# Section boundaries of a two-network kernel rebuilt: early modulation sums, GpSimd held back, first units fed by parts of h

## The reference

```python
def first_block(x, c, ...):
    cond = jax.nn.silu(c)
    for l in range(2):
        m = (cond @ w_mod[l] + b_mod[l]).reshape(bsz, 3, 3, 1024)   # shift, scale, gate for 3 sublayers
        x = x + 0.5 * m[:, 0, 2] * swiglu(adaln_in(x, norm_g[l, 0], m, 0), w1, w3, w2)   # d_ff 2752
        h = adaln_in(x, norm_g[l, 1], m, 1) @ w_in[l]
        mix = mixer_ab(h, ...) if l % 2 == 0 else mixer_cd(h, ...)
        x = x + m[:, 1, 2] * (mix @ w_out[l])
        x = x + 0.5 * m[:, 2, 2] * swiglu(adaln_in(x, norm_g[l, 2], m, 2), w1, w3, w2)

def second_block(x, c, ...):
    for l in range(2):
        sh_m, sc_m, g_m, sh_f, sc_f, g_f = split(silu(c) @ w_mod[l] + b_mod[l], 6)
        x = x + g_m * mixer(rms_norm(x) * (1 + sc_m) + sh_m, ...)
        x = x + g_f * moe_ffn(rms_norm(x) * (1 + sc_f) + sh_f, ...)   # 64 experts of width 256, top 8, and a shared one
```

## Time and profile before

| | us |
|---|---|
| median of 3 runs | 4393.25 |
| lowest and highest | 4388.53, 4394.18 |
| span of the profiled execution | 4386.6 |
| PE busy in it | 4127.6 (94%) |
| DVE, ACT, POOL busy | 2587.6, 1470.3, 990.2 |

### The profile page before, as it was taken

One profiled execution on the slowest core, in us unless ns is written; L12 is line 12 of the kernel. 1 busy time (PEld: TensorE's weight loads), 2 busy tenths in 40 slices (PEclk: granted clock), 3 DMA queues, 4 the chain that ended last, 5 costly groups with the idle time before them and its releaser, 6 DMA issues.

```text
span 4386.6 us, 74944 instructions
## 1 busy us (share of the span) xinstructions
PE 4127.6 (94%) x29877; PEld 3940.1 (90%) x29877; DVE 2587.6 (59%) x3637; ACT 1470.3 (34%) x2008; POOL 990.2 (23%) x640
## 2 busy tenths in 40 slices
PE   4998998987999888999999999998899999999999
PEld 2996898975998777999999999987789999999999
DVE  6754576655755645855555555547345555555555
ACT  1332333321331132333333333311323333333333
POOL 3827465552737104500000000061000000000000
PEclk9999898998999998999999999999989999999999
DMA  6765575752766324765656556563235565565654
GB/s 239 245 197 177 176 248 187 238 187 76 242 222 211 125 83 138 257 194 185 191 191 188 190 189 190 192 219 115 85 118 182 189 196 184 189 194 185 190 192 140
DMA packets 569485, 804.84 MB, mean 183 GB/s; under 512 B 20973, under 2 KB 487860, under 8 KB 568100
## 3 DMA queue, kind: packets, MB, share of 16 engines
q1 hardware_dynamic: 514364, 665.69, 47.2%
q0 software_dynamic: 31104, 113.26, 7.9%
q10 hardware_dynamic: 23912, 24.44, 1.7%
HBM read 802.13 MB, written 1.20 MB: 183 GB/s over the span
## 4 chain that ended last, share of the span: by engine, by line
PE 87%; DVE 10%; ACT 1%; issue 1%; DMA 1%; SPq 0%; ACTq 0%; DVEq 0%
PE bank L728 23%; PE bank L729 23%; PE bank L730 23%; PE bank L802 9%; DVE work L1785 3%; PE bank L1010 2%; PE bank L722 1%; DVE pb L1696 1%; PE bank L712 1%; DMA ring<-in_w_mod 0%; DVE h L1525 0%; PE bank L996 0%; DVE work L1639 0%; DMA ring<-in_ffn_w 0%; PE bank L824 0%
## 5 line engine op out<-in xcount | busy, mean ns | idle before, releaser
L728 PE MATMUL bank<-hh,hi 128*128 128x256 f32 (+1 forms) x5568 | 1588.5, 285 | 32.2 <-DVE h_lo L1545 30.1
L729 PE MATMUL bank<-h_lo,hi 128*128 128x256 f32 (+1 forms) x5568 | 1585.0, 285 | 0.0
L730 PE MATMUL bank<-hh,ring_lo 128*128 128x256 f32 (+1 forms) x5568 | 1584.7, 285 | 0.0
L728 PEld LDWEIGHTS bank<-hh,hi 128*128 128x128 f32 (+1 forms) x5568 | 1073.3, 193 | 38.6 <-DVE h_lo L1545 24.2
L729 PEld LDWEIGHTS bank<-h_lo,hi 128*128 128x128 f32 (+1 forms) x5568 | 1074.3, 193 | 0.0
L730 PEld LDWEIGHTS bank<-hh,ring_lo 128*128 128x128 f32 (+1 forms) x5568 | 1073.9, 193 | 0.0
L1556 DVE TENSOR_TENSOR ring_lo<-ring,hi 128x1024 fp32r<-128x1024 f32 (+1 forms) x696 | 861.1, 1278 | 76.8 <-ACT hi L1141 76.7
L728 PE MATMUL bank<-hid,hi 128*128 128x256 f32 (+1 forms) x2784 | 789.0, 283 | 3.3 <-DVE hid_lo L1588 3.3
L729 PE MATMUL bank<-hid_lo,hi 128*128 128x256 f32 (+1 forms) x2784 | 788.7, 283 | 0.0
L730 PE MATMUL bank<-hid,ring_lo 128*128 128x256 f32 (+1 forms) x2784 | 788.6, 283 | 0.0
L1141 ACT ACTIVATE hi<-ring 128x1024 fp32r<-128x1024 f32 (+1 forms) x696 | 693.1, 1044 | 210.7 <-DMA ring<-in_ws 102.7
(11 more groups left out here) (255 smaller groups left out, 3046.6 us busy)
## 6 DMA issues: line engine op xcount, KB each, us to landing
ring<-in_w SPq DMA_DIRECT2D x384, 1024.0 KB, 5.7
ring<-in_ffn_w SPq DMA_DIRECT2D x120, 1024.0 KB, 6.5
wmod<-in_w_mod POOLq DMA_DIRECT2D x216, 512.0 KB, 4.5
ring<-in_w_in SPq DMA_DIRECT2D x74, 1024.0 KB, 5.4
ring<-in_w_out SPq DMA_DIRECT2D x16, 1024.0 KB, 5.1
work<-gates_scratch ACTq DMA_DIRECT2D x128, 128.0 KB, 5.2
ring<-in_w_mod SPq DMA_DIRECT2D x12, 1024.0 KB, 14.5
ring<-in_ffn_w SPq DMA_DIRECT2D x12, 768.0 KB, 4.8
```

Of the source, the lines that this page charges most:

```text
L728: pe.matmul(o, w_hi, x_hi, start=start, stop=False, skip_group_check=True)
L729: pe.matmul(o, w_hi, x_lo, start=False, stop=False, skip_group_check=True)
L730: return pe.matmul(o, w_lo, x_hi, start=False, stop=stop, skip_group_check=True)
```

## The change

- The modulation sums are a function of their own, `sum_mods(n)`. Those of section s + 1 run in section s: before the last two units of an ffn or moe section, after the attention of sections 1 and 4, before the output projection of sections 6 and 8. All 24 columns go to bank 3 and are signalled once. Only section 0's stay behind its norm. DVE makes all modulation columns and the gain before it waits for the root.
- GpSimd starts the products for section n once section n - 1's h is complete (`h_ready`), and if that is a moe section once its gates are turned.
- The first unit's up matmuls (`first_up`) go by part k of h: both tiles and both halves for the first four parts, then the first tile's halves for the other four, then the second tile's.
- The last down signals `sums_done` behind each of its first three banks, and DVE updates the first six tiles of x on these. The squares are laid into `sq` rotated by four tiles.
- Section 3 is "early" and `joined` to section 2: it begins at slot 0, its first tile's weight parts are made beside section 2's last tiles, the others once section 2's last but one down has ended.
- The counts of `hi_done` and `lo_done` follow (`first_counts`, `down_count`). The loops on GpSimd are written out.

```diff
+        sums_done = sem("sums_done")
...
-                   "early": s in (2, 5, 7, 9)}
+                   "early": s in (2, 3, 5, 7, 9)}
             if kind in ("ffn", "moe"):
-                ringplan.align(3)
+                ringplan.align(0 if s == 3 else 3)
...
+        def joined(s):
+            return s + 1 < SECTIONS and plan[s]["kind"] == "ffn" and plan[s + 1]["kind"] == "ffn"
+
+
+        def first_counts(sec):
+            base, n = sec["half0"], 1 if sec["s"] and joined(sec["s"] - 1) else 0
+            return (base + 1 - n, base + 2 - n), (base + 3, base + 4), base + 5
...
         def down_count(sec, u6, t, last=False):
-            return u6 + (sec["half0"] + (5 + 3 * t - 2 * last))
+            early = 2 if last and not joined(sec["s"]) else 0
+            return u6 + (sec["half0"] + (5 + 3 * t - early))
...
                 fetch(0)
                 fetch(1)
-                pool.wait_ge(mod_summed, s * 2 + 2)
-                for n in range(3 * KD):
-                    third, k = n // KD, n % KD
+                pool.wait_ge(mod_summed, n)
+                pool.wait_ge(h_ready, KD * n)
+                if plan[n - 1]["kind"] == "moe":
+                    pool.wait_ge(gates_turned, (n - 1 - 6) // 2 + 1)
+                for j in range(3 * KD):
+                    third, k = j // KD, j % KD
...
                 for k in range(KD):
                     pe.wait_ge(sq_done, KD * s + k + 1)
-                    ins = pe.matmul(bank[2][:, 0:T], M["ones"], sq[:, k, :], start=(k == 0), stop=(k == KD - 1))
+                    ins = pe.matmul(bank[2][:, 0:T], M["ones"], sq[:, (k + 4) % KD, :], start=(k == 0), stop=(k == KD - 1))
                 ins.then_inc(ms_done, 1)
 
-                if s == 0:
+            def sum_mods(n):
+
+                if n == SECTIONS:
+                    return
+                if n == 0:
                     pe.wait_ge(first_mod, KD)
                     pe.wait_ge(first_gate, KD)
                     pe.wait_ge(columns_done, len(GROUPS))
                 else:
-                    pe.wait_ge(mod_step, 3 * KD * s)
+                    pe.wait_ge(mod_step, 3 * KD * n)
                 for j in range(MODT):
-                    ins = pe.matmul(bank[3 if j < 2 * KD else 1][:, j:j + 1], macc[:, j * P:(j + 1) * P], M["ones"][:, 0:1], start=True, stop=True)
-                    if j in (2 * KD - 1, MODT - 1):
-                        ins.then_inc(mod_summed, 1)
+                    ins = pe.matmul(bank[3][:, j:j + 1], macc[:, j * P:(j + 1) * P], M["ones"][:, 0:1], start=True, stop=True)
+                ins.then_inc(mod_summed, 1)
...
 
-            def down(slot, t, split, taken, rows=P, first=False):
+            EARLY_K = 4
+
+            def first_up(sec, m):
+
+
+                slots, counts = [q[0] for q in sec["slabs"][0]], first_counts(sec)
+
+                def part(k, t, half):
+                    return three(bank[t][0:m, half * T:(half + 1) * T], up_hi(half, t, m)[:, k, :], up_half(slots[half], t, m, ring_lo)[:, k, :],
+                                 hh[:, k, :], h_lo[:, k, :], k == 0 and half == 0, k == KD - 1)
+
+                for k in range(KD):
+                    pe.wait_ge(h_split, sec["split0"] + k + 1)
+                    for t in (0, 1) if k < EARLY_K else (0,):
+                        for half in (0, 1):
+                            if k == 0:
+                                pe.wait_ge(lo_done, counts[t][half])
+                            ins = part(k, t, half)
+                ins.then_inc(up_done, 1)
+                for k in range(EARLY_K, KD):
+                    for half in (0, 1):
+                        ins = part(k, 1, half)
+                ins.then_inc(up_done, 1)
+
+            def down(slot, t, split, taken, rows=P, first=False, last=False):
                 pe.wait_ge(hid_done, taken)
                 pe.wait_ge(lo_done, split)
                 w, w_hi = down_half(slot, t, rows, ring_lo), down_hi(t, rows)
...
+                    if last and m in (1, 3, 5):
+                        ins.then_inc(sums_done, 1)
...
-                up(slot, 0, lambda j: sec["half0"] + 1 + j, rows, ready=sec["split0"])
-                up(slot, 1, lambda j: up_count(sec, 0, j, 1), rows)
+                first_up(sec, rows)
                 if moe:
                     turn_gates(X)
-                down(slot[2], 0, down_count(sec, 0, 0), t0 + 1, rows, first=True)
+                down(slot[2], 0, first_counts(sec)[2], t0 + 1, rows, first=True)
                 up(odd, 0, lambda j: up_count(sec, 6, j, 0))
...
-                    down(even[2], 1, down_count(sec, u6 + 12, 1, last), tile + 4)
+                    down(even[2], 1, down_count(sec, u6 + 12, 1, last), tile + 4, last=last)
 
                 with pe.Fori(0, n // 2 - 1) as i:
                     two_units(i, False)
+                sum_mods(s + 1)
                 two_units(n // 2 - 1, True)
 
...
                     long_conv(X, taken0)
                 pe.wait_ge(*X("o_taken", 4))
+                sum_mods(s + 1)
                 pe.wait_ge(*X("conv", CT))
...
                             if m % 2:
                                 ins.then_inc(proj_done, 1)
+                sum_mods(s + 1)
...
                 norm(sec["s"])
+                if sec["s"] == 0:
+                    sum_mods(0)
...
-                    act.activation(sq[:, k, :], x[:, k, :], ACT.Square).then_inc(sq_done, 1)
+
+                    act.activation(sq[:, (k + 4) % KD, :], x[:, k, :], ACT.Square).then_inc(sq_done, 1)
...
-            def first_halves(sec):
+            def first_halves(sec, part=None):
                 m = REST_T if sec["kind"] == "ffn" else P
                 slots, counts = [q[0] for q in sec["slabs"][0]], [q[1] for q in sec["slabs"][0]]
-                split_up(slots, 0, lambda j: counts[j], m)
-                split_up(slots, 1, None, m)
-                split_down(slots[2], 0, None, counts[2], m)
+                if part != 1:
+                    split_up(slots, 0, lambda j: counts[j], m)
+                if part != 0:
+                    split_up(slots, 1, None, m)
+                    split_down(slots[2], 0, None, counts[2], m)
 
...
+                    elif joined(sec["s"]):
+                        first_halves(plan[sec["s"] + 1], 0)
                     split_down(even[2], 1, tile + 2)
                     if moe and not last:
                         act.wait_ge(hid_done, tile + 2)
                         load_gates(sec, 0, i * 2 + 2)
                     silu_tile(1, tile + 3)
+                    if last and joined(sec["s"]):
+                        act.wait_ge(down_done, tile + 3)
+                        first_halves(plan[sec["s"] + 1], 1)
                     if not last:
...
+                dve.wait_ge(mod_summed, s + 1)
+                then(dve.tensor_tensor(m[:, :], bank[3][:, 0:MODT], vec[:, bg, ba:ba + MODT], ALU.add))
+                if s < 6 and s % 3 != 1:
+                    then(dve.tensor_scalar(m[:, 2 * KD:], m[:, 2 * KD:], 0.5, None, ALU.mult))
+                then(dve.scalar_tensor_tensor(out=gain[:, s % 2, :], in0=m[:, KD:2 * KD], scalar=1.0, in1=vec[:, gg, ga + row * KD:ga + (row + 1) * KD],
+                                              op0=ALU.add, op1=ALU.mult))
                 dve.wait_ge(std_done, s + 1)
                 dve.reciprocal(rstd[:, :], std[:, :]).then_inc(rstd_done, 1)
-                dve.wait_ge(mod_summed, 2 * s + 1)
-                then(dve.tensor_tensor(m[:, 0:2 * KD], bank[3][:, 0:2 * KD], vec[:, bg, ba:ba + 2 * KD], ALU.add))
-                then(dve.scalar_tensor_tensor(out=gain[:, s % 2, :], in0=m[:, KD:2 * KD], scalar=1.0, in1=vec[:, gg, ga + row * KD:ga + (row + 1) * KD],
-                                              op0=ALU.add, op1=ALU.mult))
                 dve.wait_ge(rstd_done, s + 1)
                 for k in range(KD):
                     dve.scalar_tensor_tensor(out=h[:, k, :], in0=x[:, k, :], scalar=gain[:, s % 2, k:k + 1], in1=rstd[:, :], op0=ALU.mult, op1=ALU.mult).then_inc(scaled_done, 1)
                     if sec["kind"] == "ffn" and k:
                         lo_h(sec, k - 1)
-                    if k == KD - 2:
...
+                    elif joined(s):
+                        first_halves(plan[s + 1], 0)
                     lo_down(even[2], 1, down_count(sec, u6 + 12, 1, last))
                     expert(1, 1)
+                    if last and joined(s):
+                        first_halves(plan[s + 1], 1)
...
                 two_units(n // 2 - 1, True)
-                dve.wait_ge(down_done, t0 + 2 * n + 2)
+                banks0 = 3 * sum(plan[r]["kind"] in ("ffn", "moe") for r in range(s))
                 for k in range(KD):
+                    if k < 6:
+                        dve.wait_ge(sums_done, banks0 + k // 2 + 1)
+                    else:
+                        dve.wait_ge(down_done, t0 + 2 * n + 2)
                     add_to_x(s, k, bank[4 + k // 2][:, (k % 2) * T:(k % 2 + 1) * T])
```

64 lines of the change are left out of this document (28 added, 36 removed).

## The result

The changed kernel takes 4399.22 us (median of 20 runs), the kernel before 4390.72 us beside it (20 runs). The ratio is 1.0024, 95% interval [1.0015, 1.0032]: slower by 0.24%, 8.5 us by the medians. The forecast was 4384 us with 0.48 on faster. The measured time lies inside the range, on the other side of no change.

The account below looks back on a forecast made before the run. TensorE, never waiting inside the loops of sections 0, 2, 3, 5, 7 and 9, was taken as the bound, with only edges winnable. Won 75.25 minus paid 65.9 gave net -9.4 from 4393.25: forecast 4384 us, range 4364 to 4403.

Parts of the forecast that it names:

- point 1: Early sums' price: 8.0 us per set in five loops, +40 us; four mixers +25.9 us; 65.9 us in all.
- points 2 to 5, 7: Edge wins: freed sums 2.8 us, bank-wise sums 2.35, first units 8.2 and 9.2, section 3 17.7, section 7 17.0.
- a stall in its loop: Early in section 7's loop: a stall of 1.6 us, counted as won within section 7's 17.0 us.
- Rival (b): GpSimd is late, so the last two units of sections 0, 2 and 5 stand 11 us each: 4417 us, chance 0.08.
- (c): VectorE's long steps aren't GpSimd's doing and holding it frees nothing, 22 us less won: 4406 us, chance 0.03.
- (a): The clock holds through the sums: 43.6 us paid, net -31.7, 4361.6 us; chance 0.08.
- a half-speed pass takes 0.16 us: Step in pricing a set of 48 sum passes: all at half clock it would take 7.7 us.
- the mixers' cover: Idle of 1.93 us in section 4, the same 2 us in 6 and 8, hides part of each set: 18.2 us paid.
- the hold booked at nothing: GpSimd's new wait, held about 9 to 12 us, with margins of 1, 6 and 4 us in sections 0, 2, 5: booked 0.
- point 6: Ring's half turn puts section 5's three loads behind section 4's last slab: 10.5 us lost, first unit wins 10.1, net -0.4.
- rival (d): Section 5's loads come one after another: 4389.5 us, no change; chance 0.11.
- point 4: First units by parts, GpSimd held: TensorE never starves again; section 0 wins 8.2 us, section 2 wins 9.2, section 5 10.1.

Follow-up runs that it names:

- runs 5: Changed kernel with GpSimd not held, starting the next products once the norm passes have run: 4458.9 us, ratio 1.0141.
- run 6: Kernel before with GpSimd's hold alone, its loops written out: 4357.6 us, ratio 0.9906.
- Run 10: Kernel before with GpSimd's hold and the early sums, nothing else of the change: 4406.0 us, ratio 1.0033.
- run 12: Kernel before with GpSimd's hold alone, its loops kept as loops: 4353.1 us, ratio 0.9904.
- run 7: Changed kernel with the first unit's up matmuls in the old order, not by parts of h: 4401.7 us, ratio 1.0023.

## Right and wrong, point by point

Forecast against the means of two profiles of either kernel, in us, with the kernel before as zero:

| | forecast | measured |
|---|---|---|
| section 0, first unit | -8.2 | -7.6 |
| section 0 to 1 | -7.3 | -7.1 |
| section 1 to 2 | -9.2 | -9.0 |
| section 2 to 3 | -17.7 | -16.7 |
| section 3 to 4 | -4.0 | -3.7 |
| section 4 to 5 | +0.4 | **+5.5** |
| section 5 to 6 | -4.2 | -4.1 |
| section 6 to 7 | -17.0 | -15.3 |
| sections 7 to 8, 8 to 9 | -5.7 | -5.0 |
| end | -2.35 | -2.5 |
| won | -75.25 | **-65.5** |
| loops of 0, 2, 3, 5, 7 | +40 | **+47.2** |
| mixers 1, 4, 6, 8 | +25.9 | **+29.0** |
| net | -9.4 | **+10.7** |

The spans differ by 7.4 us only, because the changed kernel's two profiles happened to reach the first norm 3.3 us sooner; that stretch is not in the table. The medians of 20 runs differ by 8.5.

**Right: the edges, and that the sums lose the clock (point 1, points 2 to 5, 7).** Eight of the nine edges came within 2 us. The 17.0 us of the edge into section 7 hold 1.6 for a stall in its loop, so the edge itself was forecast at 15.4 and met; the stall is taken up below. GpSimd was never late: TensorE does not wait for it at any early set. Rival (b) fell for that reason, (c) by runs 5 and 6, (a) by the windows.

**Wrong: the size of a set (point 1).** The step "a half-speed pass takes 0.16 us" failed. The forecast's own row says otherwise: 9 instructions in the 2 us from 910. 0.16 us is what a whole set gives in the edge from section 0 to 1 before the change, 7.66 us for 48 passes, but that set was not all at half clock. The windows over it, kernel before:

```profile
312.50:315.50 3.00, 3.00 (x28) 3.00 (x27) 1.75 (x1) 0.47 (x1) 0.00 (x0) 0.97 0.00 0
315.50:320.50 5.00, 5.00 (x23) 4.98 (x24) 3.49 (x11) 2.80 (x7) 0.06 (x1) 0.50 0.00 0
```

More than half of the passes ran in its first 3 us, at full clock; behind them they stand 0.21 us apart, as they do at 0.50 in the changed kernel. Section 1's set, at half clock from start to end, shows it whole: 10.40 us for 48, where 7.7 were booked. In section 0's loop the clock fell after 2.3 us, and 8.14 us for the set and 2 for the tail make the 10.1. Over the eight ffn loops profiled a set came to between 6.9 and 10.1 us, 9.25 in the mean for 8.0 booked: 5.0 us over four loops. Section 7's loop paid 10.2, some 7.3 of it for the set and 2.9 in waits for VectorE, of which the next paragraph tells.

**Wrong: the mixers' cover (point 1) and the hold booked at nothing.** The sum is off by only 3 us, and that is luck: two errors nearly cancel. The hold alone (run 6) makes the mixers of sections 1, 4, 6 and 8 longer by 5.2, 5.3, 1.6 and 3.4 us, 15.5 that the forecast put at nothing. What the changed kernel adds to that is 4.0, 4.2, 0.3 and 5.0, 13.5 us for the 25.9 booked for the sums. Run 10 beside run 6, which differ by the sums alone, makes it 1.2, 5.3, 7.7 and 6.0, or 20.2; section 6's mixer, 360.2 to 372.7 us over the profiles, is what leaves it open between 13 and 20. Either way the mixers hide more of a set than was booked: section 1's takes 10.40 us and costs its mixer 1 to 4. The hold also lengthens the waits in section 7's loop, from 1.6 us before to 5.7 with the hold alone and 5.0 and 4.0 in the changed kernel's two profiles, where the forecast had the 1.6 us vanish. The waits view over that loop, first profile:

```profile
PE bank L742 <- DVE hid_lo L1637: 5.0, 5, 2.2
```

The forecast had asked whether GpSimd would be late, not over which steps of VectorE it would lie next. Together with the edges the hold still wins 35 to 41 us by the medians (runs 6 and 12).

**Wrong: the ring (point 6).** The mechanism stood: three loads behind the last freed slot. Its size was missed: forecast 10.5 us lost with the first unit winning 10.1, or 0.4 net; measured, the edge lost 5.5 net, 5.1 more. The chain of the changed kernel (start, us, what) has the two missing terms:

```profile
1091.36 9.98 DMA ring<-in_ffn_w
...
1104.57 6.35 PE bank L723 x16
```

The last load landed 11.0 us behind the last projection matmul (10.5 in the second profile), not 9; copy and split then took 2.25 us more, as before the change. And TensorE, idle for so long, ran the norm passes at 0.50: 6.35 us (5.85 in the second), where 3.5 were booked. The two terms together make 4 to 5 of the 5.1 us. The windows over the idle stretch and the passes behind it:

```profile
1092.00:1104.00 12.00, 0.00 (x0) 0.00 (x0) 5.20 (x7) 5.69 (x7) 0.00 (x0) 0.54 1.07 305
1104.00:1109.00 5.00, 4.43 (x10) 3.54 (x11) 3.24 (x11) 3.16 (x8) 0.00 (x0) 0.50 1.00 356
```

The clock was already low in the stretch without work, and the passes began at that level. The edge came out near the price of rival (d), +5.9 us, but not by its mechanism: the loads overlapped (4.9, 10.6 and 13.8 us from issue to landing, least, median and most), and 2.4 to 2.9 us of the miss are the slow norm passes.

**Wrong: what part of the change wins (point 4).** "First units part by part, GpSimd held" was costed as one item. The item's total is right and its credit was misplaced: held alone, GpSimd gives 6 of section 0's 7.6 us and 6 of section 2's 9.0 (run 6; with its loops kept, run 12, 5 and 2); the order by parts gives 1 to 2 (run 7). Likewise in section 3 the hold alone gives 12.6 of the 16.7, and early weights, bank signals and early sums share the rest.

**In sum** the gains fell 10 us short (5.1 of them at one edge, 1.6 the stall in section 7) and the price was 10 us too low: 5 for sets in the ffn loops, 2 in section 7's loop, 3 in the mixers. A forecast of 75 won and 66 paid has its sign from a difference of 9, and an error of an eighth on either side turns it. The range, made from the bounds of the terms, held; the chances leaned on the middle values too much.

## What to carry to other kernels

Work put on the bounding engine inside a saturated loop is paid in full, and 1-column matmuls in a row more than in full (7 to 10 us for 5.2 us of work); where it must stand there, put wide matmuls between, and otherwise leave it at the edge, where part of it is hidden. Before anything is moved for an engine "with time to spare", ask which steps of the critical engine it will lie over: starting GpSimd 1 to 24 us later was worth 35 to 41 us, more than all other parts together, although it cost 12 to 15 in the mixers. A ring that skips slots for alignment can set a section's first load behind the slot freed last; check that slot whenever the turn of a ring changes.
